# A second-layer PEER stage whose first expert rows are fetched and multiplied beside the product-key search

## The reference

```python
def block(xc):                                # 128 tokens
    q = (xc @ wq).reshape(C, 8, 2, 128)       # 8 heads, 2 halves
    s = einsum('chzd,zkd->chzk', q, subkeys)  # 128 keys each half
    top_s, top_i = top_k(s, 16)
    cand_s = top_s[:, :, 0, :, None] + top_s[:, :, 1, None, :]
    best_s, best_j = top_k(cand_s, 16)        # 16 experts a head
    idx = take(cand_i, best_j)
    g = softmax(best_s)
    ue, ve = u[idx], v[idx]                   # 128 rows of u and of v a token
    act = gelu(einsum('cd,chkd->chk', xc, ue))
    return einsum('chk,chkd->cd', g * act, ve)
```

## Time and profile before

| what | us |
|---|---|
| median of 3 runs | 4784.03 (4774.42 to 4784.29) |
| the profiled execution | 4783.03 |
| its span in the trace | 4781.4 |
| PE, DVE, ACT, POOL busy | 4179.8, 3339.1, 1307.1, 1767.5 |
| second layer: key steps | 3427 to 3552 |
| second layer: opening | 3557 to 3626 |
| second layer: lots | 3626 to 3905 |
| second layer: dense loop | 3930 to some 4747 |

### The profile page before, as it was taken

The page is one execution under the profiler, slowest core; times in us unless marked ns, Lnnn a source line. Parts: engine busy times, 40 slices in busy tenths (PEclk is TensorE's granted clock), DMA queues, the critical chain, the costliest instruction groups (busy, mean ns, idle before and its releaser), DMA issues.

```text
span 4781.4 us, 53394 instructions
## 1 busy us (share of the span) xinstructions
PE 4179.8 (87%) x18407; PEld 2873.7 (60%) x18407; DVE 3339.1 (70%) x6731; ACT 1307.1 (27%) x2628; POOL 1767.5 (37%) x1652
## 2 busy tenths in 40 slices
PE   7999976694999899999999979886657779999997
PEld 3676664483676666666666645553443446666665
DVE  2466665568889677777777846775588767777776
ACT  3231311111666211111111123331214652222222
POOL 0012111022665455566565600000126655454452
PEclk8999978797999999999999989998778989999998
DMA  6966774713999999999999926888518999999995
GB/s 235 286 198 200 228 224 140 262 58 106 360 408 346 389 363 400 396 389 390 368 390 391 392 99 189 227 222 233 181 52 320 381 365 398 391 389 400 394 393 224
DMA packets 514579, 1408.04 MB, mean 294 GB/s; under 512 B 45693, under 2 KB 128893, under 8 KB 509471
## 3 DMA queue, kind: packets, MB, share of 16 engines
q1 hardware_dynamic: 330014, 733.73, 46.0%
q0 software_dynamic: 184320, 671.17, 36.2%
HBM read 1226.46 MB, written 178.26 MB: 294 GB/s over the span
## 4 chain that ended last, share of the span: by engine, by line
PE 65%; DVE 14%; DMA 10%; ACT 3%; POOL 3%; issue 3%; SPq 0%; DVEq 0%; ACTq 0%; POOLq 0%
PE ps L1840 20%; PE ps L1831 17%; DMA peer_arena<-in_peer_u 4%; PE ps L1804 3%; PE ps L1518 3%; DMA u_rows<-mixer_arena 3%; PE ps L746 3%; PE ps L1227 2%; PE ps L1232 2%; DMA expert_rows<-u_rows,peer_arena 2%; PE ps L321 2%; PE ps L749 2%; DVE expert_rows L2085 2%; PE ps L815 1%; DMA u_rows<-hidden 1%
## 5 line engine op out<-in xcount | busy, mean ns | idle before, releaser
L1787 POOL DMA_INDIRECT expert_rows<-u_rows,peer_arena x640 | 829.1, 1296 | 1052.5 <-DVE expert_rows L2085 821.8
L1831 PE MATMUL ps<-part_arena,peer_part_arena 128*128 128x384 f32 (+1 forms) x4096 | 1031.4, 334 | 37.7 <-DVE peer_part_arena L2128 25.4
L2085 DVE SCALAR_TENSOR_TENSOR expert_rows<-expert_rows,mixer_in 128x1024 f32<-128x1024 f32 x640 | 762.2, 1220 | 114.3 <-DMA expert_rows<-u_rows,peer_arena 112.0
L1794 POOL DMA_INDIRECT expert_rows<-in_peer_v,peer_arena x640 | 742.5, 1160 | 223.9 <-issue 186.5
L1831 PEld LDWEIGHTS ps<-part_arena,peer_part_arena 128*128 128x128 f32 x4096 | 699.7, 190 | 110.1 <-issue 99.0
L1840 PE MATMUL ps<-best,peer_arena 128*128 128x512 f32 x1540 | 685.3, 592 | 0.0
L1831 PE MATMUL ps<-mixer_in_parts,peer_part_arena 128*128 128x384 f32 (+1 forms) x2048 | 633.7, 309 | 0.0
L2110 DVE SCALAR_TENSOR_TENSOR peer_arena<-expert_rows,peer_arena 128x1024 f32<-128x1024 f32 x445 | 571.7, 1285 | 35.0 <-DVE peer_arena L2110 1.9
L1804 PE MATMUL ps<-expert_rows,peer_arena 128*128 128x512 f32 x768 | 387.8, 653 | 202.9 <-ACT peer_arena L1919 202.7
L1840 PEld LDWEIGHTS ps<-best,peer_arena 128*128 128x128 f32 x1540 | 285.1, 189 | 296.0 <-issue 296.0
L1571 POOL TENSOR_TENSOR part_arena<-peer_arena,part_arena 128x1024 fp32r<-128x1024 f32 x32 | 76.5, 2392 | 1007.1 <-ACT part_arena L1548 1007.1
(11 more groups left out here) (273 smaller groups left out, 6104.7 us busy)
## 6 DMA issues: line engine op xcount, KB each, us to landing
peer_arena<-in_peer_u SPq DMA_DIRECT2D x256, 512.0 KB, 12.1
best<-in_peer_v SPq DMA_DIRECT2D x154, 512.0 KB, 8.2
mixer_arena<-in_peer_u SPq DMA_DIRECT2D x272, 256.0 KB, 7.4
u_rows<-mixer_arena SPq DMA_DIRECT2D x136, 512.0 KB, 5.0
hidden<-in_peer_u SPq DMA_DIRECT2D x240, 256.0 KB, 6.2
u_rows<-hidden SPq DMA_DIRECT2D x120, 512.0 KB, 5.1
gates<-peer_arena SPq DMA_DIRECT2D x20, 2048.0 KB, 10.7
peer_arena<-in_peer_v SPq DMA_DIRECT2D x52, 512.0 KB, 7.6
```

The source lines that it names most:

```text
L1787: pool.indirect_dma_start(u_ring[:, k % U_SLOTS, :], None, u_table, bass.IndirectOffsetOnAxis(u_index[s][:, m:m + 1], 0)).then_inc(u_row_i ...
L1794: pool.indirect_dma_start(v_ring[:, k % V_SLOTS, :], None, v_table, bass.IndirectOffsetOnAxis(v_index[s][:, m:m + 1], 0)).then_inc(v_row_i ...
L1831: mm = pe.matmul(ps[:, 6, 0:dense_tok], left[j % len(left)][:, c, :], right[:, c, :], start=at == 0, stop=at == len(todo) - 1)
L2085: dve.scalar_tensor_tensor(out=rows, in0=rows, scalar=1.0, in1=B.x[:, :, rows_at + s * P:rows_at + s * P + P], op0=ALU.mult, op1=ALU.mult, ...
```

## The change

In the second layer `product_keys` is replaced by `keys_and_rows`: the same 16 steps written out, with a part of `peer`'s work between them. After step 3 DVE runs `choose` for heads 0 and 1 of the first sparse tile. From step 5 on DVE does one group of products a step (11 groups, 22 rows), from step 7 shares (8 groups); from step 10 ACT and PE write diagonals and sum one group a step (6 groups, 12 rows). POOL gathers the first 26 u rows and 16 v rows in this stage, into slots of their own (`u_early`, `v_early`, 4 each). The stage clears 8 more semaphores. `peer` then starts at row 22: its `choose(0)` does the 6 other heads in one part instead of 8 in two, its pieces too have products between them, and 8 groups instead of 6 stand before `turn(0)`; `groups_beside` spreads the remaining 29 groups over the 64 lots. SP no longer loads `iota` at its start. The dense loop is as it was. The first layer keeps the loop; there only ACT's second exponential moves from before the fourth of the 6 opening groups to behind the sixth. Functions inside `peer` that both stages need (`search`, `decode`, the index arithmetic, the tiles' places) move to the top of the file unchanged.

```diff
+Early = collections.namedtuple("Early", "heads groups gelus shares sums u_rows v_rows")
+EARLY = (Early(0, 0, 0, 0, 0, 0, 0), Early(2, 11, 8, 8, 6, 26, 16))
+CHOSEN_BEHIND, EARLY_FROM = 3, 5
+U_EARLY, V_EARLY = 4, 4
...
-            keys = make(product_keys, layer, segs)
+            keys = make(keys_and_rows if EARLY[layer].heads else product_keys, layer, segs)
...
+def keys_and_rows(B, layer, segs):
...
+    def group_at(j):
+
+        return j - EARLY_FROM
...
+        for j in range(STEPS):
+            if j + 1 < STEPS:
+                project(j + 1)
+            score(j)
+            if group_at(j) >= 5:
+                spread(group_at(j) - 5)
...
+        for j in range(STEPS):
+            take(j)
+            if j + 2 < STEPS:
+                split_w(j + 2)
+            if j == CHOSEN_BEHIND + 1:
+                exp()
+            if group_at(j) >= 3:
+                gelus(group_at(j) - 3)
+            if group_at(j) >= 5:
+                diagonals(group_at(j) - 5)
...
+        def gather_u(a):
+            if a == 0:
+                pool.wait_ge(index_ok, 1)
+            for k in range(GROUP * a, GROUP * a + GROUP):
+                if k >= U_EARLY:
+                    pool.wait_ge(score_ok, k - U_EARLY + 1)
...
+        def gather_v(a):
+            for k in range(GROUP * a, GROUP * a + GROUP):
+                if k >= V_EARLY:
+                    pool.wait_ge(s0_mm, k - V_EARLY + 1)
...
+        for j in range(STEPS):
+            split_low(j)
+            if group_at(j) >= 1:
+                gather_u(group_at(j) - 1)
+            if group_at(j) >= 6:
+                gather_v(group_at(j) - 6)
+        for a in range(group_at(STEPS) - 1, E.u_rows // GROUP):
+            gather_u(a)
+            if a < 13:
+                gather_v(a - 5)
...
+        for j in range(STEPS):
+            strongest(j)
+            if j == CHOSEN_BEHIND:
+                choose()
+            if group_at(j) >= 0:
+                products(group_at(j))
+            if 0 <= group_at(j) - 2 < E.shares:
+                shares(group_at(j) - 2)
...
 def peer(B, layer, segs):
...
-    AHEAD = 6
+    E = EARLY[layer]
+    AHEAD_AT = (0, 3, 5, 8, 10, 13, 15, 18) if E.heads else (16, 18, 20, 22, 24, 25)
+    AHEAD, EXP_FIRST = len(AHEAD_AT), 3 if E.heads else 0
+    G0, K0, SUMMED = E.groups, GROUP * E.groups, GROUP * E.sums
+    late, PARTS = slice(E.heads, HEADS), 1 if E.heads else 2
...
-        return range(AHEAD + (FIRST - AHEAD) * lot // BATCH, AHEAD + (FIRST - AHEAD) * (lot + 1) // BATCH)
+        at = G0 + AHEAD
+        return range(at + (FIRST - at) * lot // BATCH, at + (FIRST - at) * (lot + 1) // BATCH)
...
     def gpsimd(pool):
-        for k in range(steps):
+        for k in range(E.v_rows, steps):
             s, m = divmod(k, PAIRS)
-            if m == 0:
-                pool.wait_ge(index_ok, s + 2 if s else 1)
-            elif k == PAIRS // 2:
+            if k == E.heads * TOPK:
+                pool.wait_ge(index_ok, 1)
+            elif k == PAIRS // 2 and PARTS == 2:
                 pool.wait_ge(index_ok, 2)
-            if k >= U_SLOTS:
-                pool.wait_ge(score_ok, k - U_SLOTS + 1)
...
-            if k >= V_SLOTS:
+            if k - V_SLOTS >= SUMMED:
                 if k - V_SLOTS < first_rows:
-                    pool.wait_ge(s0_mm, k - V_SLOTS + 1)
+                    pool.wait_ge(s0_mm, k - V_SLOTS + 1 - SUMMED)
...
-        for a in range(AHEAD - 1):
+        for a in range(E.sums, G0 + AHEAD - 1):
             spread(a)
         turn(0)
...
-        exp(0)
-        for a in range(AHEAD):
-            if a == 3:
-                exp(1)
+        for a in range(E.gelus, G0):
             gelus(a)
-            if a:
-                diagonals(a - 1)
+        for a in range(E.sums, G0 - 1):
+            diagonals(a)
+        for n in range(AHEAD):
+            if n == EXP_FIRST:
+                exp(0)
+            gelus(G0 + n)
+            if G0 + n:
+                diagonals(G0 + n - 1)
+        exp(1)
...
-        dve.wait_ge(iota_in, 16)
-        for _ in choose(0):
-            pass
+        if not E.heads:
+            dve.wait_ge(iota_in, 16)
         ahead = 0
-        for piece, _ in enumerate(choose(1)):
-            if piece in (0, 2, 4, 6, 8, 9):
-                products(ahead)
-                if ahead:
-                    shares(ahead - 1)
+        for piece, _ in enumerate(itertools.chain(choose(0), choose(1))):
+            if piece in AHEAD_AT:
+                products(G0 + ahead)
+                for a in range(G0 + ahead - 1 if ahead else E.shares, G0 + ahead):
+                    shares(a)
                 ahead += 1
```

460 lines of the change are left out of this document (340 added, 120 removed).

## The result

The changed kernel takes 4752.65 us, the median of 5 runs (4748.98 to 4758.55), against 4784.03 for the kernel before (5 runs beside it, 4774.42 to 4786.35): ratio 0.9948, 95% interval 0.9937 to 0.996. Run again later, it took 4760.3 against 4780.4, ratio 0.9958 (0.9942 to 0.9974). So it is faster by some 20 to 31 us. The profiled execution took 4752.65 us with a span of 4750.7, 30.7 less than before.

What follows compares the result with a forecast made beforehand. DVE was taken to bound the key steps, DMA the lots, PE and DMA the dense loop. From 4783.0 us, 40.5 - 1.8 + 1.2 - 63 + 1 = -22.1 gave 4761 us; 8-in-10 range 4739 to 4795.

Steps and rivals of the forecast that it cites:

- Key steps: Second layer's key steps on DVE: choice +10.3, products and shares +26.5, loop written out -3.0, PE's sums +2.5.
- rival B: Key steps: POOL's subtraction blocks DVE's products, price 24 us; 4785 us, no change; chance 0.12.
- nothing beyond what the 110.1 already holds: Key steps, 110.1 us before: no added cost for POOL's subtraction beside DVE; upper end 24 us.
- The stage's end: Boundary after the key steps: last gathers +3.5, 8 more semaphores at most +0.7, no `iota` load -1.8.
- three issues of 0.94 and their gaps: Key stage's end: POOL's last u gather and two v gathers after the last product, +3.5 us.
- The opening: Start of `peer` up to the copy: 69.7 us against 68.5 before, +1.2, including 7.3 for u row 26.
- rows 26 and 27 land at about 21.5: Opening: u rows land then, DVE wants them at 13.1 and leaves them at 22.8 instead of 15.5 us.
- The lots: Second layer's lots: 13 groups fewer free 31.9 us of DVE; 219 us instead of 282, -63.
- The wait w: Lots: DVE's wait for u rows, taken as 25 us against 56.1 before.
- Rival A: Lots: waits come with writes, not the number of rows; w = 64, 4800 us, 0.3% slower; chance 0.13.
- Rival C: Key steps run at PE's and POOL's pace, 10.6 us a step instead of 8.8; 4776 us; chance 0.13.
- The first layer and the dense loop: First layer: ACT's moved exponential makes DVE wait, +1 us; dense loops: nothing.

Runs made afterwards that it cites:

- written-out kernel: Changed kernel with the 16 key steps written out but choice, products, shares, sums and row fetches left to `peer`: 4768.5 us, ratio 0.9983.
- without early sums: Changed kernel with no rows summed on PE beside the keys and only 4 v rows fetched early: 4771.1 us, ratio 0.9988.
- the one with u rows earlier: Changed kernel with u rows 26 to 31 put before v rows 20, 22 and 26 in POOL's `peer` queue: 4750.9 us, ratio 0.9944.
- the version with the u rows first: Changed kernel with 24 u and 14 v rows early, u rows 24 and 25 first in POOL's `peer` queue: 4758.2 us, ratio 0.9949.

## Why the forecast came out, point by point

4761 was forecast, 8.3 us above the first median and 0.7 above the second; the range and the direction held, and so did the chain of the argument: rows and DVE work moved to a stretch where DMA is idle, paid in full by DVE there, given back with interest in the lots. That the sum came so close is in part luck: its terms were off by up to 13 us, and the errors went both ways. What the sum does not show is that 10.3 of the 25.4 us come from the loop written out; beyond it the rows beside the keys bring 15.1 us (476.2 against 461.1), or 11.0 by the repetition.

- **Key steps**, +34.1 for +36.3. The choice took 10.3, as forecast; the other 3.0 of its step's 13.3 are the slow L1984. Eleven groups at 2.15 (8.25 less DVE's own 6.10) and eight shares at 0.07 are 24.2, not 26.5. Writing out is worth 8.9 in a kernel of its own, not 3.0, but 6.8 of that are the four collisions: I priced the loop by two steps of the earlier trace rows and left the others unread, three of which were stretched. DVE waited 5.0 us for PE, not 2.5. The rest, some 2 the other way, is that DVE's own step is 6.10 where the written-out kernel runs at PE's 6.37.
- **The subtraction beside the products** (rival B): no product lasts over 1.226 us, so the queue order protects them, as argued. But the same order puts the subtraction beside the end of DVE's step, and L1984 took 3.09, 1.40 and 1.48 us instead of 0.20. That is 5.4 us of collisions, against 6.8 in the kernel before: "nothing beyond what the 110.1 already holds" came out in the sum, but with new collisions in place of the old ones, which I had not foreseen. In the repetition five instructions are slow, 7.2 us, and DVE waits 3.4 for PE instead of 5.0; so in the steps that PE bounds a collision costs next to nothing.
- **The stage's end**, +9.0 for +2.4 (+3.5, +0.7, -1.8). The step that failed is the term "three issues of 0.94 and their gaps", which ends with the issues: POOL's drain lasts 6.4 us beyond the last of them, about as long as a gather takes to land.
- **The opening**, +7.9 for +1.2. The wait for row 26 and its cause were right, and so was the time at which the queue comes to it: v row 25 was issued 14.5 us after DVE's start (3610.92), forecast 14.4, and DVE wanted the row at 13.3 (3609.72), forecast 13.1. What failed was "rows 26 and 27 land at about 21.5": row 26 came at 22.3, 6.5 us after its issue at 3612.17, and row 27, which stands a v row further back, 2.5 us later, so that DVE left the pair at 26.0 instead of 22.8. The other half of the miss is small: 1.1 for a stall of the kind told of below, 1.0 more for PE before the copy, some 1.4 in gaps.
- **The lots**, -76.3 for -63. DVE's work fell by 31.5 (219.7 to 188.2), as forecast (31.9). The wait w was 15.6 for 25, and the remaining 4.3 lie outside both. Rival A, that waits come with writes alone, is refuted by 15.6 against its 64, though the writes do make half of them before and two thirds after. I took the middle between scaling by groups (39) and the first layer's density (11); the density was the better guide.
- **Rival C**: steps of 9.5 to 9.8 from step 9 on, between my 8.8 and its 10.6. The first two of them are DVE's own with a slow L1984, the rest PE's, whose projection, scores and sum take 9.80 by themselves. Rows that land late have a part in it, PE's two waits for v rows of 7.9 us in all; it waited longer, 13.2 us, for POOL's subtraction, which stood behind gathers.
- **The first layer and the dense loop**: -3.9 ahead of the stage and -1.4 behind it are run-to-run, as the 14 traces show. Of the 30.7 us in the spans, 25.4 belong to the change (21 by the repetition's stretch).

## What to carry to other kernels

Work moved into a stretch with idle DMA pays by the waits that it removes where DMA is full: these fell from 56.1 to 24.6 us with the first seven groups and by 9 more with the next four, which as a whole brought 0 to 4 us. Run the new structure without the moved work too: here writing the loop out was over a third of the gain. Before pricing a move by one step of a loop, list every step's period; a few stretched ones may hold more than the whole difference looked for, and look for the same collision in the new kernel, where it can sit beside another instruction. When one wait is removed from a chain whose queue is shared, look for which row is late next: here three edits each removed the named wait and the opening stayed within some microseconds, or got longer.

## What the runs showed of the hardware that I had not expected

- A drain of POOL lasts beyond the issue of its gathers, until their rows have landed as far as seven traces show: the last traffic and the drain's end lie 1.6 to 2.2 us apart in them (3591 and 3593.05 in the changed kernel, 3585.1 and 3586.8 without early sums). DVE's next stage starts 8.7 to 10.2 us after the last gather is issued, in the changed kernel 6.4 to the drain's end and 3.4 for the clearing of semaphores. An engine may be done long before.
- POOL's subtraction holds up also a DVE instruction with one input (L1605, 0.20 us alone, 1.72 to 1.77 beside it; L1984 up to 3.09), and such a collision came again in each of the next three steps. It goes the other way too: a u gather that starts during a product takes 1.68 to 1.77 us on POOL, else 0.94.
- DVE's chained short instructions, 2.4 us for the eleven of the decoding, took 9.7 in one kernel of the same work, with up to 1.8 us between two (and 3.2 before a product). The kernel before has no such stall in this stretch, the changed one 1.1 us, its repetition some 8 us, the one with u rows earlier 8.7, the version with the u rows first 14. They come while POOL issues gathers back to back and DMA is full (share 1.01), but gathers at the same pace stood beside the fast decoding too. What releases DVE there stays open.
- Why the last opening microseconds differ between two runs of the same kernel (76.4 and 79.7) is left open with it.
